# A fourth of the first block's low weight halves by accumulating transfers, and the gb slabs in three passes

## The reference

```python
h = x @ w_in[l] + b_in[l]
conv_a, conv_g, q, k, v, r, f_lr, gate_a, gate_b = jnp.split(h, split_points, axis=-1)
y_conv = conv_module(conv_a, conv_g, ...)     # u = a * sigmoid(g); 31-tap causal convolution; LayerNorm; silu; @ w_co
y_gla = gla_branch(q, k, v, r, f_lr, ...)     # gated linear attention over chunks of 64; norm; silu(r); @ w_o
merged = jax.nn.sigmoid(gate_a) * y_conv + jax.nn.sigmoid(gate_b) * y_gla
x = layer_norm(ALPHA * x + merged @ w_out[l] + b_out[l], ln1_g[l], ln1_b[l])
x = layer_norm(ALPHA * x + hier_moe(x, ...), ln2_g[l], ln2_b[l])   # 64 experts, two for each token
```

## Time and profile before

| | |
|---|---|
| median of 3 runs | 1693.7 us (1693.39 to 1693.9) |
| the profiled execution | 1691.89 us, of which its span is 1689.8 |
| TensorE, products | 1364.6 us, 81% of the span |
| VectorE | 674.2 us, 40% |
| ScalarE | 472.0 us, 28% |
| GpSimd | 59.0 us, 3% |
| memory transfers | 530.79 MB, 314 GB/s over the span, all by SyncE's queue but for the instructions |

### The profile page before, as it was taken

How to read it: one execution, slowest core, us unless ns; L and a number is a source line. 1 busy time by engine, 2 the same in 40 slices (tenths; PEclk the granted TensorE clock), 3 DMA queues, 4 the chain that set the end, 5 groups by cost and what they waited for, 6 DMA issues and landing times.

```text
span 1689.8 us, 21326 instructions
## 1 busy us (share of the span) xinstructions
PE 1364.6 (81%) x8600; PEld 883.5 (52%) x8600; DVE 674.2 (40%) x1109; ACT 472.0 (28%) x682; POOL 59.0 (3%) x27
## 2 busy tenths in 40 slices
PE   8999999976656666665666667566799999999998
PEld 7789988522212212221221222122499999778887
DVE  5787979311101100110111011001367888655874
ACT  4454233401001001010010010010265764546653
POOL 0000000670000000000000000000000000000000
PEclk9999999988787978887888888788999999999999
DMA  9433555899999999999999999999944325474440
GB/s 359 156 138 138 218 204 245 353 431 430 432 431 431 431 433 433 431 431 432 433 433 431 431 432 433 431 432 431 419 165 150 139 71 197 167 258 175 179 174 25
DMA packets 50441, 530.79 MB, mean 314 GB/s; under 512 B 4276, under 2 KB 5556, under 8 KB 33862
## 3 DMA queue, kind: packets, MB, share of 16 engines
q1 hardware_dynamic: 50374, 529.86, 75.8%
HBM read 528.80 MB, written 1.05 MB: 314 GB/s over the span
## 4 chain that ended last, share of the span: by engine, by line
PE 51%; DMA 39%; DVE 6%; ACT 3%; issue 1%; SPq 0%; DVEq 0%; ACTq 0%
DMA shared<-in_w 37%; PE psum L454 6%; PE psum L456 6%; PE psum L455 6%; PE psum L1433 6%; PE psum L367 5%; PE psum L2222 4%; PE psum L1456 4%; PE psum L2223 2%; PE psum L1462 2%; PE psum L1404 2%; PE psum L2059 1%; DVE ring_parts L590 1%; DMA arena<-in_w 1%; PE psum L611 1%
## 5 line engine op out<-in xcount | busy, mean ns | idle before, releaser
L1433 PE MATMUL psum<-ring,arena 128*32 128x512 f32 x992 | 145.3, 739 | 86.8 <-DMA ring<-in_w 86.6
L1433 PE MATMUL psum<-shared,arena 128*32 128x512 f32 x1040 | 151.0, 726 | 61.5 <-DMA shared<-in_w 61.4
L1665 DVE TENSOR_TENSOR shared<-shared,psum 128x512 f32<-128x512 f32 x16 | 11.0, 688 | 462.3 <-PE psum L1433 462.3
L1456 PE MATMUL psum<-shared 128*32 128x512 f32 x512 | 89.5, 834 | 68.4 <-DMA shared<-in_w 68.4
L454 PE MATMUL psum<-parts 128*128 128x256 f32 (+1 forms) x424 | 136.5, 322 | 0.7 <-DVE parts L532 0.7
L455 PE MATMUL psum<-parts 128*128 128x256 f32 (+1 forms) x424 | 135.1, 319 | 0.0
L1433 PEld LDWEIGHTS psum<-ring,arena 128*32 128x32 f32 x992 | 34.3, 132 | 185.3 <-DMA ring<-in_w 100.2
L456 PE MATMUL psum<-parts,ring_parts 128*128 128x256 f32 x464 | 131.2, 283 | 0.0
L1433 PEld LDWEIGHTS psum<-shared,arena 128*32 128x32 f32 x1040 | 38.2, 129 | 168.3 <-issue 91.8
L456 PE MATMUL psum<-parts 128*128 128x256 f32 (+1 forms) x392 | 126.1, 322 | 0.0
L454 PE MATMUL psum<-parts,ring_parts 128*128 128x256 f32 x400 | 114.8, 287 | 0.4 <-ACT shared L2256 0.4
(11 more groups left out here) (343 smaller groups left out, 2347.4 us busy)
## 6 DMA issues: line engine op xcount, KB each, us to landing
shared<-in_w SPq DMA_DIRECT2D x47, 4096.0 KB, 32.4
ring<-in_w SPq DMA_DIRECT2D x47, 4096.0 KB, 32.4
ring<-in_w_in SPq DMA_DIRECT2D x19, 2048.0 KB, 8.7
ring<-in_w_ffn_gate_up SPq DMA_DIRECT2D x11, 2048.0 KB, 8.2
ring<-in_w_gate SPq DMA_DIRECT2D x8, 2048.0 KB, 7.9
ring<-in_w_ffn_down SPq DMA_DIRECT2D x5, 2048.0 KB, 7.8
ring<-in_w_out SPq DMA_DIRECT2D x4, 2048.0 KB, 8.6
shared<-in_w SPq DMA_DIRECT2D x6, 1024.0 KB, 28.8
```

Source lines behind the costliest of these rows:

```text
L1433: m = pe.matmul(ps[slots, bank, :], V.picked[:, k, slots], w[e * len(w) // QUAD][:, e % (QUAD // len(w)), j, :], start=(k == 0), stop=(k = ...
L1456: m = pe.matmul(ps[slots, MOE_BANK["down"][c], :], V.hidden_t[:, f, slots], w(e), start=(f == 0), stop=(f == ET - 1))
```

## The change

- **Every fourth unit's low half comes by a transfer.** For n with n % 4 = 3, the last unit of each slab, ScalarE writes the negated high half into the low buffer (signal in_minus) and then the high half. GpSimd's program, which was empty in the first block, waits for in_minus and issues a transfer that reads the unit's 512 KB of weights from memory once more and adds them to the buffer (`add_low`). VectorE skips the low of these 13 units; TensorE waits for the transfer's signal, low_added.
- **A fourth buffer pair.** `BUFS` is 4. The transferred units use a place of their own: slot 9 up to unit 43, then slot 6. ScalarE's copies may be four units ahead instead of three.
- **gb0 and gb1 join the three passes** as units 44 to 51, their sigmoids join ScalarE's loop. The drain for moe_read0 moves behind gb1, `norm_heads` moves into iterations 45 and 46, and gla_in is signalled after iteration 51.
- **Paces and places on VectorE.** A transferred unit's iteration has 6 taps instead of 4; the other work moves one iteration later.
- **SyncE** waits, before it loads over a slab, for the copy of its last unit and the lows of the other three, instead of the last low.
- The host stores these slabs of `w_in` unit by unit, so that a unit is 4 KB in one piece for each partition. Two signals of the router, group_exp and expert_exp, become one.

The core of the diff:

```diff
-    SLABS = ["g0", "a1", "g1", "k", "v0", "v1", "q", "r0", "r1", "ga0", "ga1"]
+    SLABS = ["g0", "a1", "g1", "k", "v0", "v1", "q", "r0", "r1", "ga0", "ga1", "gb0", "gb1"]
-    BUFS = 3
+    BUFS, BY_DMA = 4, 3
+    LATE = 4 * SLABS.index("gb0")
...
-        return self.K.parts(12 + n % self.BUFS, 1024, 1024 * low).rearrange("p (k n) -> p k n", k=k)
+        slot = 12 + n % self.BUFS
+        if self.by_dma(n):
+            slot = 9 if n < self.LATE else 6
+        return self.K.parts(slot, 1024, 1024 * low).rearrange("p (k n) -> p k n", k=k)
...
+        if self.by_dma(n):
+            L.done(L.eng.activation(self.part(n, 1), src, ACT.Copy, scale=-1.0), self.K.sem("in_minus"))
         L.done(L.eng.activation(self.part(n, 0), src, ACT.Copy), self.K.sem("in_high"))
+    def add_low(self, pool, n):
+        slab, i = self.SLABS[n // 4], n % 4
+        pool.wait_ge(self.K.sem("in_minus"), n // self.BUFS + 1)
+        src = self.K.d["w_in"][IN_SLABS.index(slab)][:, 1024 * i:1024 * i + 1024]
+        pool.dma_start(self.part(n, 1).rearrange("p k n -> p (k n)"), src, accum_op=ALU.add)\
+            .then_inc(self.K.sem("low_added"), 16)
...
-        eng.wait_ge(self.K.sem("in_low"), n + 1)
+        if self.by_dma(n):
+            eng.wait_ge(self.K.sem("in_high"), n + 1)
+            eng.wait_ge(self.K.sem("low_added"), 16 * (n // self.BUFS + 1))
+        else:
+            eng.wait_ge(self.K.sem("in_low"), self.lows(n))
...
     slab_tiles("ga1", "ga", 4)
+    for s in range(2):
+        slab_tiles(f"gb{s}", "gb", 4 * s)
     pe.drain().then_inc(S("moe_read0"), FREED)
-    for s in range(2):
-        pe_slab_tiles(K, pe, B, R, f"gb{s}", tiles("gb", 4 * s, 4), x)
...
-        split.low(L, n)
+        by_dma = split.by_dma(n)
+        if not by_dma:
+            split.low(L, n)
-        pace = 0 if done < 0 else 2 if done < 4 or 8 <= done < 12 else 4
+        pace = 0 if done < 0 else 2 if done < 4 or 8 <= done < 12 else 6 if by_dma else 4
...
-    for pair in range(2):
-        norm_heads(pair)
     dve.sem_inc(S("gla_conv"), 1)
...
-            split.wait_low(sp, split.unit(before) + 3)
+            last = split.unit(before) + 3
+            sp.wait_ge(S("in_high"), last + 1)
+            sp.wait_ge(S("in_low"), split.lows(last))
```

More of the change, by code:

```diff
@@ L348, in rstd, with first_slab_at @@
         return self.A(2, T, 1024 if i == 3 else 240 + T * i)
+    def first_slab_at(self, slot):
+        return self.ring_cols(slot * SLOT_COLS, SLOT_COLS).rearrange("p (m k n) -> p m k n", m=4, k=DT)
     def first_slab(self, ring):
-        return self.ring_cols(ring.slot("a0") * SLOT_COLS, SLOT_COLS).rearrange("p (m k n) -> p m k n", m=4, k=DT)
+        return self.first_slab_at(ring.slot("a0"))
     def slab(self, slot, k=DT):
@@ L503, in part, with by_dma, lows @@
         k = 2 if self.SLABS[n // 4] in self.ROWS else DT
-        return self.K.parts(12 + n % self.BUFS, 1024, 1024 * low).rearrange("p (k n) -> p k n", k=k)
+        slot = 12 + n % self.BUFS
+        if self.by_dma(n):
+            slot = 9 if n < self.LATE else 6
+        return self.K.parts(slot, 1024, 1024 * low).rearrange("p (k n) -> p k n", k=k)
+    def by_dma(self, n):
+        return n % self.BUFS == self.BY_DMA
+    def lows(self, n):
+        return n + 1 - (n + 1) // self.BUFS
     def source(self, eng, n):
         slab, i = self.SLABS[n // 4], n % 4
-        w = self.K.slab(self.K.ring1.wait_landed(eng, slab))
-        return w[:, 2 * i:2 * i + 2, :] if slab in self.ROWS else w[:, :, i * P:(i + 1) * P]
+        slot = self.K.ring1.wait_landed(eng, slab)
+        if slab in self.ROWS:
+            return self.K.slab(slot)[:, 2 * i:2 * i + 2, :]
+        return self.K.first_slab_at(slot)[:, i]
     def wait_read(self, eng, n):
@@ L736, in block1_pe @@
         b = B.take(pe, f"co{n}")
-        pe.wait_ge(S("in_low"), end.FIRST + n + 1)
+        pe.wait_ge(S("in_low"), end.FIRST_LOW + n + 1)
         w = end.part(n, 0), end.part(n, 1)
@@ L876, in outputs @@
             evac(f"ga{m}", K.tiles(8, DT)[:, m, :], ACT.Sigmoid, bias=K.v("b_ga", m))
+        elif slab in ("gb0", "gb1"):
+            m = i + 4 * int(slab[2])
+            evac(f"gb{m}", K.tiles(9, DT)[:, m, :], ACT.Sigmoid, bias=K.v("b_gb", m))
     kdec, o = K.tiles(10, TT, GDK, TT * GDK), K.tiles(4, DT)
@@ L904, in block1_act @@
                    B, "o_ms")
-    for m in range(DT):
-        evac(f"gb{m}", K.tiles(9, DT)[:, m, :], ACT.Sigmoid, bias=K.v("b_gb", m))
     end = EndSplit(K)
@@ L1060, in block1_dve @@
             gate(done - 4)
-        if n == 22:
+        if n == 23:
             log_decay()
-        elif n == 27:
+        elif n == 28:
             keys_decayed()
[L1065 to L1068, removed]
+        elif n in (31, 33, 35, 37):
+            next_state((n - 31) // 2)
+        elif n in (40, 41):
+            for m in range(4 * (n - 40), 4 * (n - 40) + 4):
                 gate_head(m)
             pace = 1
-        elif n == 41:
+        elif n in (45, 46):
+            norm_heads(n - 45)
+            pace = 1
+        elif n == 42:
             B.wait_read(dve, "o_ms")
@@ L1504, in moe_act @@
         L.done(act.activation(W.gexp[:, t, :], W.logits[:, t, 0:NG], ACT.Exp, bias=W.group_max[:, t:t + 1],
-                              accum_out=W.gsum[:, t:t + 1]), S("group_exp"))
+                              accum_out=W.gsum[:, t:t + 1]), S("router_exp"))
     act.wait_ge(S("expert_below"), 1)
     for t in range(TT):
-        L.done(act.activation(W.eexp[:, t, :], W.masked[:, t, :], ACT.Exp, bias=W.expert_max[:, t:t + 1]), S("expert_exp"))
+        L.done(act.activation(W.eexp[:, t, :], W.masked[:, t, :], ACT.Exp, bias=W.expert_max[:, t:t + 1]), S("router_exp"))
     for t in range(TT):
         L.done(act.activation(W.top2_exp[:, t, :], W.top8[:, t, 0:2], ACT.Exp, bias=W.expert_max[:, t:t + 1],
-                              accum_out=W.sums[:, t:t + 1]), S("expert_exp"))
+                              accum_out=W.sums[:, t:t + 1]), S("router_exp"))
     act.preload_act_table(ACT.Sqrt)
@@ L1708, in moe_dve, with block1_pool @@
     L.done(dve.tensor_scalar(u_rows[:, 1, :], x2[:, 1, :], K.stat("rstd", 1), None, ALU.mult), S("u_rows1"))
+def block1_pool(K, pool):
+    split = InSplit(K)
+    for n in range(split.BY_DMA, split.units, split.BUFS):
+        split.add_low(pool, n)
 def moe_pool(K, pool):
@@ L1714, in moe_pool @@
     step, V = S("pool_steps"), moe_views(K)
-    pool.wait_ge(S("group_exp"), TT)
-    pool.wait_ge(S("expert_exp"), 2 * TT)
+    pool.wait_ge(S("router_exp"), 3 * TT)
     L.done(pool.tensor_tensor(W.sums, W.sums, W.gsum, ALU.mult), step)
@@ L2947, in host_arrays @@
     out["w_in"] = np.stack([by_partition(w[:, IN_COLS[n]:IN_COLS[n] + 512]) for n in IN_SLABS])
+    for i, n in enumerate(IN_SLABS):
+        if n not in InSplit.ROWS:
+            out["w_in"][i] = out["w_in"][i].reshape(P, DT, 4, P).transpose(0, 2, 1, 3).reshape(P, SLOT_COLS)
     out["w_in_first"] = np.stack([by_partition(w[:, O_A + m * P:O_A + (m + 1) * P]) for m in range(4)])
@@ L2996, in _ @@
         def _(pool):
+            block1_pool(K, pool)
             moe_pool(K, pool)
```

2 lines of the change are left out of this document (1 added, 1 removed).

## The result

The changed kernel takes **1715.18 us** (median of 4 executions, 1710.51 to 1719.30); the kernel before took 1693.55 beside it (1693.11 to 1693.90). The ratio is 1.0129, with a 95% interval of 1.0115 to 1.0144: 21.6 us slower. That is outside the range of 1688 to 1707, on the side of the first rival. The profiled execution is the one of 1710.51, with a span of 1708.7; the other three are 4 to 9 us longer and have no trace.

A forecast was written before the change was run, and what follows sets the result against it. TensorE and VectorE arriving together at the convolution's mean were taken to bound the kernel. A gain of 1.1 us there, less 0.8 for the clock and no transfer stalls, gave 1693.4 us from 1693.7; range 1688 to 1707.

The forecast's parts named there:

- the first rival: Transfers land late, sharing the way with a 2 MB slab load; at 10.5 us landing 12 us slower, 1705; chance 0.25.
- The transfers: From negated copy to landing 6.5 us, against 7.6 us left by TensorE at unit 7, 6.7 at 23: no stall.
- a pause of 3.5 us: TensorE, done with go0 at 220.7, waits 3.5 us for VectorE's last tap before the convolution's mean.
- The rest costs nothing: ScalarE's 21 more copies (22 us), the fourth buffer and the later expert, mem and co0 loads were to cost nothing.
- gb in three passes: TensorE's gb products, 192 instructions at 2.88 us a unit, take 23.0 us: 4.7 us gained, go0 ended at 220.7.
- VectorE's tail: After unit 50's low at 194.7, 74 taps take 29.4 us and end at 224.1; the mean gains only 1.1 us.
- The clock behind that wait: TensorE's half clock after its 3.5 us wait slows the mean by 0 to 1.7 us; 0.8 taken.
- the sum: 1.1 us gained at the mean and 0.8 lost to the clock: -0.3 on 1693.7, giving 1693.4 us.
- Starved descriptors: Rival: GpSimd cannot write descriptors while VectorE works; landing 9.4 us, 6.3 us slower, 1699.7; chance 0.05.
- TensorE's whole 4.7 us: Rival: last tap already at 220.7 by a shorter start of VectorE's tail, so all 4.7 us arrive, 1689.0; chance 0.13.

The follow-up runs named there:

- paced kernel: Changed kernel with negated copies three units ahead and 9 taps instead of 6 in every fourth unit from 23 to 47: 1690.33 us, 0.9988 of the kernel before.
- The kernel with the early start: Changed kernel with the negated copy of every fourth unit made three units ahead, into two alternating places: 1696.89 us, 1.0026 of the kernel before.
- the control: The kernel before, unchanged, profiled once more to check its start: 1692.34 us.

## Why the prediction was wrong, step by step

- **The transfers: the step that failed.** The landing was taken as 6.5 us, near the rows of 4.9 and 7.1. For a transfer alone that is right: 5.7 to 6.5. But the prediction itself had put the slab's load 1 us behind, and its 6.5 has no price for company; only its rival had. In company it is 8.0 to 9.5, and in the crowds at units 3, 7 and 51 10.5 to 13.4, beyond the row of 10.5 that was the upper bound. The slack was right at units 7, 11 and 51 (at unit 23 it was some 8, not 6.7): unit 7 waited 3.5 us, and 39.36 + 10.51 against the forecast slack of 7.6 from the end of the negated copy (39.07) gives 3.2.
- **Two units were misjudged.** Unit 3 was put among those with more slack; it goes out among the loads of the start and costs 2.1. Unit 51 was given unit 7's slack and a pause of 3.5 us to hide in. Its landing is the longest, since VectorE's signal lets the loads of mem, gain and co0 go at the same moment, 210.64 to 211.74. The prediction had moved these loads behind the end of the loop under "The rest costs nothing"; they cost the transfer 7.5 us, and its wait of 6.4 fills that pause and more.
- **The first rival**, at 12 us for a landing of 10.5, was what happened, and still too cheap: 14.2 us of waits and 4.6 at half clock, less the 4.7 of gb. The clock behind a wait in the middle of the stage was in no term.
- **gb in three passes: right.** Units of 2.88 us, 4.5 us earlier at the mean in the paced kernel.
- **VectorE's tail: right.** 74 taps, 29.38 us; where the transfers come in time TensorE waits 3.34 us for it (3.5 forecast).
- **The clock behind that wait: mis-sized.** Bounds of 0 to 1.7, taken 0.8; measured 1.79 behind 3.34 us, and 1.71 and 1.79 behind waits of 3.35 and 3.33 in the two runs with no slab beside the transfers. It is a little over the upper bound. With 1.8 in its place the sum is +0.7, not -0.3. The kernel with the early start, which has just this end and no late transfer, is 1.4 behind the control there and 4.5 behind the kernel before in the end; the difference is the stretch behind the experts.
- **Starved descriptors: false**, by two runs, the write in place of the add and half the bytes. VectorE's work was the same where the landing halved.
- **TensorE's whole 4.7 us: false for this change, reachable.** It needed a shorter tail, as the rival said, and timely transfers; the taps had room in VectorE's idle 20 us.

The Trainium skill (DMA: Bandwidth & Descriptors, "Anatomy of one DMA — SWDGE (gpsimd) path") gave 3.2 us by estimate for this transfer without the accumulation. The trace has 4.0 to 4.3 for it, alone, so the measurement decides; by either figure a plain transfer would not have stalled units 7 to 47, and the adding one did.

## What to carry to other kernels

Price a transfer by what leaves at the same moment: an event that frees a buffer often releases several loads, and the one with the least slack should go first or earlier than the event. A transfer that adds is to be counted at up to twice a plain one (8.0 to 9.5 us against 4.1 to 4.4 beside a slab load, 5.7 to 6.5 against 4.0 to 4.3 alone), and its lead is worth more than its size. When an engine's saving is to be kept, look at the other engine that arrives at the same place, and move its work forward into the gaps it has, before the first is made faster.

## What the runs showed of the hardware

- A 512 KB transfer of GpSimd's queue that adds to its target takes 3.3 us of the 16 engines and lands in 5.7 to 6.5 us with no slab load beside it; one that only writes takes 1.8 and lands in 4.0 to 4.3. GpSimd's issue is 0.86 us against 0.53.
- A slab load of 2 MB issued about 1 us behind adds 2 to 3 us to the first and 0.1 to the second. Among several loads both are late: 10.5 to 13.4 and 10.1 to 12.1 us.
- After 3.3 us without a product TensorE's next 16 products of the mean took 5.3 to 5.4 us, after 5.4 us 6.3 to 6.4, in place of 3.62.
- The start of an execution varies: x between 6.46 and 7.21 us, and the first 6 to 12 products behind it (in the first trace of before and in the control) at steps of 0.43 us, where later ones go at 0.22, though the rows give a granted clock of 1.00; the first unit was read at 24.98 to 27.00.
